# The first layer's four gate tiles as seven block products each, with their weight sums on GpSimd and their product sums on VectorE, and other hand-overs between stages

## The chip, the cores and the metric

The kernel runs on one core of a Trainium2 chip. The core has five engines that run side by side, each through its own instructions in order: TensorE (in the rows PE for its products and PEld for its weight loads), VectorE (DVE), ScalarE (ACT), GpSimd (POOL) and SyncE (SP), which here starts the transfers. The engines wait for one another by semaphores. The metric is the device time of one execution in microseconds (us); lower is better. All data are fp32, and in the rows every product of the program stands as two PE records, each with its own weight load.

## The reference, cut to what matters

Three different layers run one after the other over one sequence of 256 tokens of width 1024. The first projects a normalised, modulated input, runs a gated delta rule (4 heads) and a blockwise attention (8 heads), and merges both branches:

```python
gate_a, gate_b = sigmoid(h @ w_in[:, 4104:5128]), sigmoid(h @ w_in[:, 5128:6152])
merged = gate_a * (y_dn @ w_proj_dn) + gate_b * (y_mb @ w_proj_mb)
x = x + post_gate * rmsnorm(merged @ w_out)
```

The second has three branches (a linear recurrence, an mLSTM and a stick-breaking attention of 4 heads of width 64), three such gates, an output projection and a gated feed-forward part. The third has a neighbourhood attention, an RWKV-7 recurrence in both directions, an attention over a memory, and an expert feed-forward part with 16 experts, whose weights (16 x 3 matrices of 1024 x 2048 fp32) are read once.

## The kernel before

Tokens stand in two halves of 128 (t = 0, 1). `k.hT` holds the normalised input channel-major as 8 chunks of 128 channels by 256 tokens. Weights come through `k.ring`, six slots of 2 MB each, and sums are formed in the eight PSUM banks of `k.ps`.

The program is a row of stages. Each stage has one block of instructions for each engine; an engine ends its part with `k.finish`, which drains it and raises a semaphore, and `k.wait_finished` waits for named engines' earlier parts. `project` runs a stage's projections tile by tile from ring slots 0 and 1 (banks 0 to 3); TensorE's part began by waiting for VectorE, ScalarE and GpSimd.

Between a layer's projections and its merge stands a stage whose products depend on each other (`delta_and_attention` in the first layer, `memory_and_sticks` in the second). While VectorE and ScalarE work between two dependent products, TensorE takes pieces of the remaining gate projections. `fill.products` is a generator of these pieces; `spend(n)` takes the next n of them at places written out by hand, and `spend(1000)` at the end takes what is left.

In the first layer the generator was that of `GateFill`: four tiles of 512 columns, each as 4 blocks of 128 columns by 8 chunks of channels, so 32 products of 256 columns (tokens), 128 in all, one to a piece. Line 871 records them. `spend` took 108 pieces ahead of `turn_y`, the last dependent product of the stage, and 20 after it. ScalarE's `fill.copy` took each pair of blocks through a sigmoid out of PSUM (line 887).

In the second layer the generator was that of `SevenFill`: a tile is a 2 x 2 by 2 x 2 block product (two halves of the channels, two halves of the tile's columns, two halves of the tokens), and is formed from seven block products, p1 to p7, for eight, by Winograd's scheme. A block product is 4 chunks of channels by 2 blocks of 128 columns by 128 tokens. One piece is two products of 128 columns, a block product 4 pieces, a tile 28 and the four tiles 112 (line 973). It needs four sums of the token halves (`TokenSums`, s1 to s4, once, on GpSimd), four sums of the weight blocks of each tile (t1 to t4, `first_sums` and `later_sums`, 128x1024 each, on VectorE, in place in the ring slot), copies of three partial sums out of PSUM (`copy_product`: p1, p3, u2, on ScalarE), and six sums of products (`c11` and the five of `ends`, 128x256 each, on VectorE). The sigmoid follows on the finished tile (`sigmoid`, 128x1024).

At the end of `delta_and_attention`, VectorE (line 1807) and ScalarE (line 1841) copied the turned rows `yT`, which the merge multiplies. `first_merge` began on TensorE with a wait for VectorE and GpSimd, ran `branch_products` (8 steps of 8 products, four banks in turn, step i from 4 on waiting until VectorE has read step i-4), and between its second and third step `gate_rows`, after a wait for ScalarE. VectorE first forms the gain from two rows that SyncE loads after the whole stage before has ended (lines 671 and 672), and then merges (`merge_branches`). The weights of the second branch come into ring slot 1 when the fill's last tile has left it.

In `memory_and_sticks`, `values` formed the sticks' output with tokens on partitions (six products of 64 columns for each pair of heads), VectorE copied it, TensorE turned it (`turn_y(7, y_s)`, line 2143), and VectorE copied the turned rows (line 2249).

Of the kernel before, what the change touches and what calls it, by code (L numbers as in the profile page):

```python
# [17 lines left out]
ALU = mybir.AluOpType  # L18
# [304 lines left out]
def project(k, hT, stream, narrow=None, vector=None, between=None, sync=None, gpsimd=None, ahead=()):  # L323
# [37 lines left out]
    def _(pe):  # L361
# [134 lines left out]
class Merge:  # L496
# [7 lines left out]
    def __init__(self, k, name, branches, w_out, slots=(0, 1, 2, 3, 4), earlier=None, order=None):  # L504
# [35 lines left out]
def branch_products(k, pe, m, fill=None, beside=None):  # L540

    nc = k.nc
    for i, (p, b) in enumerate(m.order):
        if i < 2 and fill:
            fill.wait_read(pe, i)
        if i == 2 and beside:
            beside()
# [9 lines left out]
        for n in range(2):  # L557
            for c in range(br["chunks"]):
                last = nc.tensor.matmul(k.ps[:, i % 4, n * S:(n + 1) * S], w[:, c, (2 * p + n) * P:(2 * p + n + 1) * P], br["rows"](c),  # L559
                                        start=c == 0, stop=c == br["chunks"] - 1)  # L560
# [6 lines left out]
def merge_branches(k, dve, m):  # L567
# [3 lines left out]
    for i, (p, b) in enumerate(m.order):  # L571
# [7 lines left out]
        sums = k.ps[:, i % 4, :].rearrange("p (c s) -> p c s", s=S)  # L579
# [70 lines left out]
def first_merge(k, m, fill, tiles, ahead):  # L650
# [28 lines left out]
    def _(pe):  # L679
# [5 lines left out]
        k.wait_finished(pe, "vector", "gpsimd")  # L685
        branch_products(k, pe, m, fill, gate_rows)
# [21 lines left out]
        project_rows(mixed_tile, 0, 0, range(DC)).then_inc(first_done, 1)  # L708
        project_rows(narrow_tile, 1, 0, range(DC // 2))
        turn_normed(k, pe, m, 1)  # L710
        project_rows(narrow_tile, 1, 0, range(DC // 2, DC)).then_inc(first_done, 1)
        pe.wait_ge(m.hT_act, m.before["hT_act"] + 2)
        pe.wait_ge(m.hT_dve, m.before["hT_dve"] + 2)
        project_rows(mixed_tile, 2, 1, range(DC)).then_inc(k.tile_done[mixed_tile["slot"]], 1)
        project_rows(narrow_tile, 3, 1, range(DC)).then_inc(k.tile_done[narrow_tile["slot"]], 1)
# [25 lines left out]
    def _(act):  # L741
# [25 lines left out]
        for t in range(TT):  # L767
# [4 lines left out]
            nc.scalar.copy(rows[:, t, :].rearrange("p (g n) -> p g n", n=S)[:, 0::2, :], k.ps[:, 2 * t, :].rearrange("p (g n) -> p g n", n=S))  # L772
# [4 lines left out]
            nc.scalar.copy(k.small[:, t, 0:8], k.ps[:, 2 * t + 1, S:S + 8])  # L777
            nc.scalar.activation(rows[:, t, S:2 * S], k.ps[:, 2 * t + 1, 0:S], ACT.Sigmoid)
# [111 lines left out]
class TokenSums:  # L890


    def __init__(self, k):
        at = k.store[:, 0:4 * DC // 2 * P].rearrange("p (s c n) -> p s c n", s=4, c=DC // 2)
        self.s1, self.s2, self.s3, self.s4 = [at[:, n] for n in range(4)]
        self.ready = k.count["pools"] + 5
# [15 lines left out]
class SevenFill(GateFill):  # L912
# [141 lines left out]
    def sigmoid(self, k, act, i):  # L1054
        gate = self.tiles[i][2]
        self.vector_done(act, i, "ends")
        k.nc.scalar.activation(gate, gate, ACT.Sigmoid)

# [3443 lines left out]
```

## Time and profile before

| | us |
|---|---|
| median of 3 runs | 1985.04 |
| lowest, highest | 1982.36, 1987.23 |
| the profiled execution's own time | 1987.0 |
| its span, first to last instruction | 1985.2 |
| TensorE busy | 1680.0 (85%) |
| VectorE busy | 528.0 (27%) |
| ScalarE busy | 307.3 (15%) |
| GpSimd busy | 11.2 (1%) |

The first 41 us are the head, the first layer ends at about 336 us of the span, the second at about 746 us, the experts' loop of the third begins at about 1085 us and lasts to the end. A row's time stamp is counted from the first instruction. Busy shares are means over stages that differ: what a change is worth is read from the chain of work and the waits of the stage in which it is made.

### The profile page before, as it was taken

The numbers are of one execution on the slowest core, as the hardware profiler recorded it, in microseconds if no ns is written. First come the engines' busy times: TensorE is split into PE (matmuls) and PEld (weight loads), VectorE is DVE, ScalarE is ACT, GpSimd is POOL, SyncE is SP. The second block draws the span as 40 slices with busy tenths as digits, with TensorE's granted clock in tenths as the row PEclk, the third lists the DMA queues.
The fourth block names the chain that finished last, engine by engine and source line by source line (L and its number), as shares of the span: only waits on it lengthen the run. The fifth ranks groups of instructions, "written<-read, shape, count | busy, mean of one in ns | idle before, by whom it ended". The sixth has DMA issues, their size and how long they took to land.

```text
span 1985.2 us, 26212 instructions
## 1 busy us (share of the span) xinstructions
PE 1680.0 (85%) x11580; PEld 1066.2 (54%) x11580; DVE 528.0 (27%) x914; ACT 307.3 (15%) x594; POOL 11.2 (1%) x14
## 2 busy tenths in 40 slices
PE   6999999999999999999999966666776675666667
PEld 4868876899699648899886422222222221221222
DVE  1424422456455462355634000000000000000001
ACT  2150303332211111231421000000000000000001
POOL 1000001000000000000000000000000000000000
PEclk9999999999999999999999988878878877878879
DMA  8632380353396225403559999999999999999998
GB/s 312 226 123 80 126 297 3 129 187 136 115 317 200 76 95 182 159 2 76 173 201 389 403 430 432 432 433 433 432 430 430 432 431 432 433 433 432 431 430 338
DMA packets 109569, 558.54 MB, mean 281 GB/s; under 512 B 14312, under 2 KB 49197, under 8 KB 95789
## 3 DMA queue, kind: packets, MB, share of 16 engines
q1 hardware_dynamic: 108857, 556.09, 69.6%
q8 instruction: 69, 1.13, 0.2%
q10 hardware_dynamic: 628, 1.20, 0.2%
q14 instruction: 15, 0.12, 0.0%
HBM read 556.22 MB, written 1.05 MB: 281 GB/s over the span
## 4 chain that ended last, share of the span: by engine, by line
PE 63%; DMA 34%; DVE 1%; ACT 1%; issue 1%; ACTq 0%; SPq 0%; DVEq 0%; POOL 0%; POOLq 0%
DMA ring<-in_w_exp_up 17%; DMA ring<-in_w_exp_down 16%; PE ps L390 13%; PE ps L2414 7%; PE ps L871 6%; PE ps L4176 6%; PE ps L4128 4%; PE ps L559 4%; PE ps L600 4%; PE ps L2660 3%; PE ps L973 2%; PE ps L398 2%; PE ps L3238 1%; PE ps L700 1%; PE ps L3989 1%
## 5 line engine op out<-in xcount | busy, mean ns | idle before, releaser
L4176 PE MATMUL ps<-ring,xn 128*32 128x512 f32 x1984 | 306.5, 773 | 168.2 <-DMA ring<-in_w_exp_up 115.1
L4176 PEld LDWEIGHTS ps<-ring,xn 128*32 128x32 f32 x1984 | 71.0, 136 | 361.8 <-issue 182.2
L390 PE MATMUL ps<-hT,ring 128*128 128x256 f32 x1104 | 246.3, 383 | 1.8 <-ACTq L208 1.5
L4128 PE MATMUL ps<-ring,hT 128*32 128x512 f32 x960 | 146.8, 765 | 102.8 <-DMA ring<-in_w_exp_down 102.4
L390 PEld LDWEIGHTS ps<-hT,ring 128*128 128x128 f32 x1104 | 208.9, 191 | 33.2 <-issue 4.6
L4297 DVE TENSOR_TENSOR hT<-hT,ps 128x512 f32<-128x512 f32 x16 | 11.0, 687 | 564.5 <-PE ps L4176 564.5
L4128 PEld LDWEIGHTS ps<-ring,hT 128*32 128x32 f32 x960 | 34.2, 135 | 204.3 <-DMA ring<-in_w_exp_down 117.7
L871 PE MATMUL ps<-hT,ring 128*128 128x256 f32 x512 | 120.5, 384 | 0.4 <-issue 0.3
L871 PEld LDWEIGHTS ps<-hT,ring 128*128 128x128 f32 x512 | 93.7, 190 | 15.5 <-issue 3.4
L3989 PEld LDWEIGHTS ps<-xn,xs 128*128 128x128 f32 x512 | 62.0, 191 | 55.3 <-issue 54.6
L4235 ACT ACTIVATE hT<-ps 128x512 f32<-128x512 f32 x16 | 9.6, 597 | 447.0 <-PE ps L4176 447.0
L559 PE MATMUL ps<-chan,ring 128*128 128x256 f32 x352 | 76.9, 380 | 1.7 <-DVEq L208 0.9
L600 PE MATMUL ps<-ring,xn 128*128 128x512 f32 x176 | 76.5, 592 | 0.0
L4301 DVE COPY xn<-ps 128x512 f32<-128x512 f32 x16 | 11.1, 691 | 239.1 <-PE ps L4128 239.1
L559 PEld LDWEIGHTS ps<-chan,ring 128*128 128x128 f32 x352 | 66.6, 190 | 12.0 <-issue 2.0
L3989 PE MATMUL ps<-xn,xs 128*128 128x32 f32 x512 | 68.9, 278 | 0.5 <-DVE xn L4335 0.5
L2414 PE MATMUL ps<-xn,chan 128*128 128x128 f32 x528 | 62.6, 275 | 0.0
L2414 PEld LDWEIGHTS ps<-xn,chan 128*128 128x128 f32 x528 | 60.7, 192 | 0.0
L4123 PE MATMUL ps<-xn 128*128 128x512 f32 x128 | 59.3, 605 | 0.8 <-ACT xn L4243 0.8
L600 PEld LDWEIGHTS ps<-ring,xn 128*128 128x128 f32 x176 | 33.2, 190 | 39.4 <-issue 39.2
L4243 ACT COPY xn<-ps 128x512 f32<-128x512 f32 x16 | 9.4, 585 | 244.4 <-PE ps L4128 244.4
L4123 PEld LDWEIGHTS ps<-xn 128*128 128x128 f32 x128 | 22.8, 189 | 38.3 <-issue 37.7
(621 smaller groups left out, 1858.3 us busy)
## 6 DMA issues: line engine op xcount, KB each, us to landing
ring<-in_w_exp_gate SPq DMA_DIRECT2D x28, 4096.0 KB, 23.4
ring<-in_w_exp_up SPq DMA_DIRECT2D x28, 4096.0 KB, 25.3
ring<-in_w_exp_down SPq DMA_DIRECT2D x27, 4096.0 KB, 23.5
ring<-in_w_in SPq DMA_DIRECT2D x27, 2048.0 KB, 7.8
ring<-in_w_ffn_in SPq DMA_DIRECT2D x11, 2048.0 KB, 8.9
ring<-in_w_exp_gate SPq DMA_DIRECT2D x7, 2048.0 KB, 10.5
ring<-in_w_ffn_out SPq DMA_DIRECT2D x5, 2048.0 KB, 14.2
ring<-in_w_exp_up SPq DMA_DIRECT2D x5, 2048.0 KB, 13.7
```

Of the source, the lines that this page charges most:

```text
L390: last = nc.tensor.matmul(k.ps[:, 2 * slot + n // 2, (n % 2) * S:(n % 2 + 1) * S], wt[:, c, n * P:(n + 1) * P], src[:, c, 0:S], start=c == ...
L398: last = nc.tensor.matmul(k.ps[:, 2 * slot + t, 0:width], src[:, c, t * P:(t + 1) * P], wt[:, c, 0:width], start=c == 0, stop=c == chunks - 1)
L559: last = nc.tensor.matmul(k.ps[:, i % 4, n * S:(n + 1) * S], w[:, c, (2 * p + n) * P:(2 * p + n + 1) * P], br["rows"](c), start=c == 0, st ...
L600: product = k.nc.tensor.matmul(k.ps[:, 4 + 2 * t + h, :], m.mixed[:, c, t * P:(t + 1) * P], k.slot(slot, D)[:, c % 4, h * BANK:(h + 1) * B ...
L871: product = k.nc.tensor.matmul(k.ps[:, self.bank(unit), n % 2 * S:(n % 2 + 1) * S], w[:, c, n * P:(n + 1) * P], k.hT[:, c, :], start=c == ...
L973: last = k.nc.tensor.matmul(out[:, h * P:(h + 1) * P], weights[:, c, h * P:(h + 1) * P], rows[:, c, :], start=fresh and (c, h) == (0, 0), ...
L2414: last = nc.tensor.matmul(out[:, h * P:(h + 1) * P], weights_of[:, c, h * P:(h + 1) * P], rows_of[:, c, :], start=fresh and (h, c) == (0, ...
L2660: last = nc.tensor.matmul(k.ps[:, bank, :], rows_of[:, c, :], f.weights(k, at, 1)[:, 0, cols(h)], start=fresh and c == 0, stop=c == KH - 1 ...
L3989: last = nc.tensor.matmul(k.ps[:, bank, c * CAP:(c + 1) * CAP], picked[:, t, c, :], hot[:, t, :], start=t == 0, stop=t == TT - 1)
L4123: nc.tensor.matmul(k.ps[:, 2 * t + h, :], way[:, t * P:(t + 1) * P], y[:, h * BANK:(h + 1) * BANK], start=False, stop=True, skip_group_che ...
L4128: last = nc.tensor.matmul(k.ps[32 * i:32 * i + 32, Y + h, :], act_t[:, i, j, :], down_row(e, 2 * GATES + j, i, opening)[:, h * BANK:(h + 1 ...
L4176: last = nc.tensor.matmul(hidden_block(j, bank), xe[:, 2 * n + cc, :], hidden_columns(slot(e, q, EFF, opening)[:, cc, :], j), start=n == 0 ...
```

## The change

- The first layer's fill becomes a `PoolSevenFill`: seven block products for eight. Its `TokenSums` are made by GpSimd in the stage of the projections, and its weight sums by GpSimd in `delta_and_attention` (`make_sums`). VectorE forms the sums of products at places written out by hand between its other work, ScalarE's copies stand at such places too, and the four sigmoids stand at the end of ScalarE's part.
- `first_merge` starts its first step when `yT` is copied (`rows_ready`), and waits for VectorE and GpSimd only ahead of the second (`opened`); the merges of layers one and two take the banks in an order in which the first step's is free early. The same in `second_merge_and_ffn`.
- `project` of layers two and three waits for ScalarE only ahead of its second part (`scalar_from=1`); the rows projected at the end of the stage before stand in banks 4 to 7 for 0 to 3, and `ffn_out` drops a wait.
- The sticks: `values` forms the output turned, by four products (two of 256 and two of 128 columns) with 64 weight columns each, so that both heads of a pair fill the two halves of the partitions in alternation. `turn_y(7, y_s)`, its copy and their waits are gone. `sticks` issues the products of a pair of heads in alternation.

```diff
 def project(k, hT, stream, narrow=None, vector=None, between=None, sync=None, gpsimd=None, ahead=(), scalar_from=0):
...
-        k.wait_finished(pe, "vector", "scalar", "gpsimd")
+        k.wait_finished(pe, "vector", "gpsimd")
         for index, part in enumerate(stream.parts):
+            if index == scalar_from:
+                k.wait_finished(pe, "scalar")
...
+class PoolSevenFill(SevenFill):
+    SUMS = {name: n + 1 for n, name in enumerate(("t1", "t2", "t3", "t4"))}
...
+    def make_sums(self, k, pool):
+        for i, (slot, before, _) in enumerate(self.tiles):
+            w = [[self.weights(k, i, kh, j) for j in range(2)] for kh in range(2)]
+            pool.wait_ge(k.w_landed[slot], 16 * (before + 1))
+            if i:
+                self.product_done(pool, i - 1, "p5")
+            k.nc.gpsimd.tensor_tensor(self.t1, w[0][1], w[0][0], ALU.subtract).then_inc(k.pools, 1)
+            self.sum_done(pool, i, "t1")
+            k.nc.gpsimd.tensor_tensor(w[0][1], w[1][1], self.t1, ALU.subtract).then_inc(k.pools, 1)
+            self.product_done(pool, i, "p2")
+            self.sum_done(pool, i, "t2")
+            k.nc.gpsimd.tensor_tensor(w[0][0], w[0][1], w[0][0], ALU.subtract).then_inc(k.pools, 1)
+            k.nc.gpsimd.tensor_tensor(w[1][0], w[1][0], w[0][1], ALU.subtract).then_inc(k.pools, 1)
...
+    def first_block(self, k, dve, i):
+        self.product_done(dve, i, "p2")
+        self.copied(dve, i, "p1")
+        self.combine(k, self.place_of(i, 0, 0), self.place_of(i, 0, 0), self.blocks(k, i, 1), ALU.add, "c11")
...
 # delta_and_attention, GpSimd
         nc.gpsimd.memset(Y(0, 8)[high, :, 0:64], 0.0).then_inc(zeroed, 1)
+        pool.wait_ge(zeroed, 1)
+        fill.make_sums(k, pool)
 # VectorE
         nc.vector.tensor_tensor(d_y, d_y, over(k.const("chunk_ident"), 8), ALU.add).then_inc(triangles, 1)
+        fill.first_block(k, dve, 0)
         invert_vector(k, dve, d_t, a21_t, d_x, d_y, d_u, Y(0, 8), whole_done)
+        fill.ends(k, dve, 0)
...
         nc.vector.tensor_reduce(s.t1, squares, AX_X, ALU.add).then_inc(out_squares, 1)
+        fill.first_block(k, dve, 1)
...
         last.then_inc(y_ready, 1)
+        fill.ends(k, dve, 1)
+        fill.first_block(k, dve, 2)
         finish(0)
         shift(2)
         shift(3)
         weigh(2)
         weigh(3)
+        fill.first_block(k, dve, 3)
+        fill.ends(k, dve, 2)
         finish(1)
         dve.wait_ge(y_turned, 1)
-        nc.vector.tensor_copy(yT[:, 0:2, :], ...)
+        nc.vector.tensor_copy(yT[:, 0:2, :], ...).then_inc(y_ready, 1)
+        fill.ends(k, dve, 3)
         k.finish(dve, "vector")
 # ScalarE: fill.copy(0..7) give way to copy_product(0..3, "p1", "p3", "u2"), and at its end
         act.wait_ge(y_turned, 1)
-        nc.scalar.copy(yT[:, 2:4, :], ...)
-        fill.copy(k, act, 6)
-        fill.copy(k, act, 7)
+        nc.scalar.copy(yT[:, 2:4, :], ...).then_inc(y_ready, 1)
+        for i in range(4):
+            fill.sigmoid(k, act, i)
         k.finish(act, "scalar")
...
 # first_merge, TensorE (banks 4 to 7 for 0 to 3 in its project_rows)
-        k.wait_finished(pe, "vector", "gpsimd")
-        branch_products(k, pe, m, fill, gate_rows)
+        pe.wait_ge(*fill.rows_ready)
+        branch_products(k, pe, m, beside=gate_rows, opened=lambda: k.wait_finished(pe, "vector", "gpsimd"))
 # second_merge_and_ffn, TensorE
-        k.wait_finished(pe, "vector", "gpsimd")
...
-        branch_products(k, pe, m)
+        branch_products(k, pe, m, opened=lambda: k.wait_finished(pe, "vector", "gpsimd"))
...
 # memory_and_sticks, TensorE
         def values(g):
             pe.wait_ge(exps, g + 1)
             for n, h in enumerate((2 * g, 2 * g + 1)):
-                c = slice(n * 64, (n + 1) * 64)
-                d = slice(P + n * 64, P + (n + 1) * 64)
-                nc.tensor.matmul(k.ps[:, 4 + 2 * g, c], z[:, h, 0:P], v(0, h), start=True, stop=True)
-                nc.tensor.matmul(k.ps[:, 4 + 2 * g, d], z[:, h, P:S], v(0, h), start=True, stop=False)
-                last = nc.tensor.matmul(k.ps[:, 4 + 2 * g, d], z[:, h, S:W], v(1, h), start=False, stop=True)
+                nc.tensor.matmul(k.ps[64 * n:64 * n + 64, 4 + 2 * g, 0:S], v(0, h), z[:, h, 0:S], start=True, stop=False, skip_group_check=True)
+            for n, h in enumerate((2 * g, 2 * g + 1)):
+                last = nc.tensor.matmul(k.ps[64 * n:64 * n + 64, 4 + 2 * g, P:S], v(1, h), z[:, h, S:W], start=False, stop=True, skip_group_check=True)
             last.then_inc(sticks_done, 1)
...
         values(1)
-        spend(9)
-        pe.wait_ge(y_copied, 2)
-        turn_y(7, y_s)
         spend(1000)
 # VectorE
-            nc.vector.tensor_copy(y_s[:, :, g * P:(g + 1) * P], ...).then_inc(y_copied, 1)
+            nc.vector.tensor_copy(yT[:, 2 + g, :], k.ps[:, 4 + 2 * g, 0:S])
...
-        dve.wait_ge(y_turned, 2)
-        nc.vector.tensor_copy(yT[:, 2:4, :], ...)
         fill.ends(k, dve, 3)
```

## Rows read from the trace of the kernel before

**Rows 1.** Page, the chain that ended last, by engine.
```profile
PE 63%; DMA 34%; DVE 1%; ACT 1%; issue 1%; ACTq 0%; SPq 0%; DVEq 0%; POOL 0%; POOLq 0%
```
**Rows 2.** Stages: from:to, length, busy of each engine (instructions), clock, DMA share.
```profile
163.80:255.60 91.80, 91.52 (x824) 77.95 (x824) 44.97 (x83) 24.29 (x54) 0.00 (x0) 1.00 0.26 93
...
409.70:475.80 66.10, 65.31 (x580) 64.06 (x580) 43.64 (x73) 28.93 (x39) 0.00 (x0) 1.00 0.56 207
```
**Rows 3.** TensorE's waits: for whom, us in total, times, longest.
```profile
PE ps L390 <- ACTq L208: 1.5, 2, 0.9
...
PE ps L559 <- DVEq L208: 0.9, 1, 0.9
...
PE ps L871 <- issue: 0.3, 1, 0.3
PE ps L973 <- issue: 0.3, 1, 0.3
```
**Rows 4.** Chain in order of time, first layer: start, us, what.
```profile
166.28 5.62 PE ps L871 x26
...
214.47 0.44 PE ps L1699 x4
...
219.66 1.02 PE ps L1709 x16
...
227.23 8.83 PE ps L871 x40
...
246.78 8.63 PE ps L871 x40
255.42 0.37 issue
```
**Rows 5.** Chain in order of time, second layer's fill.
```profile
411.30 1.51 PE ps L2095 x16
412.81 6.45 PE ps L973 x56
...
459.86 0.17 PE ps L2135 x2
...
460.92 0.22 PE ps L2137 x2
461.14 6.31 PE ps L973 x56
...
472.81 0.45 PE ps L2143 x4
```
**Rows 6.** GpSimd in order of time: start, us, operation, shape [idle before].
```profile
336.66 1.26 POOL L905 TENSOR_TENSOR store<-hT 128x512 f32<-128x512 f32 x1
```
**Rows 7.** VectorE in order of time, first and second layer.
```profile
171.17 0.69 DVE L1750 TENSOR_TENSOR ring<-ring,constants 128x512 f32<-128x512 f32 x1
...
196.52 0.69 DVE L1754 COPY ring<-ps 128x512 f32<-128x512 f32 x1 [2.86 <-PE ps L1655]
...
203.00 0.69 DVE L1765 TENSOR_TENSOR ring<-xn 128x512 f32<-128x512 f32 x1
...
425.61 0.42 DVE L1013 TENSOR_TENSOR store<-store,ps 128x256 f32<-128x256 f32 x1 [0.58 <-PE ps L973]
```
**Rows 8.** ScalarE in order of time, a sigmoid of the second layer's fill.
```profile
438.42 1.28 ACT L1057 ACT_TABLE_LOAD   x1
439.71 1.06 ACT L1057 ACTIVATE tok<-tok 128x1024 f32<-128x1024 f32 x1
```
**Rows 9.** First merge: SyncE in order of time, the issue of a row.
```profile
256.60 0.43 SPq L672 DMA_DIRECT2D tok<-in_g_post  x1
```
**Rows 10.** First merge: VectorE in order of time.
```profile
266.72 1.22 DVE L722 TENSOR_TENSOR tok<-tok,ps 128x1024 f32<-128x1024 f32 x1 [19.21 <-DMA tok<-in_g_post]
...
269.12 1.28 DVE L582 TENSOR_TENSOR xn<-ps,tok 128x512 f32<-128x512 f32 x2
```
**Rows 11.** Third layer and experts, stretches as in rows 2.
```profile
980.00:1020.00 40.00, 40.00 (x243) 33.52 (x242) 15.47 (x31) 16.82 (x32) 0.00 (x0) 1.00 0.26 93
...
1060.00:1080.00 20.00, 20.00 (x79) 12.67 (x78) 6.21 (x10) 3.05 (x9) 0.00 (x0) 1.00 1.00 424
```

More of the change, by code:

```diff
@@ L320, in ahead, with project @@
         return loads
-def project(k, hT, stream, narrow=None, vector=None, between=None, sync=None, gpsimd=None, ahead=()):
+def project(k, hT, stream, narrow=None, vector=None, between=None, sync=None, gpsimd=None, ahead=(), scalar_from=0):
     nc = k.nc
@@ L545, in branch_products @@
             fill.wait_read(pe, i)
+        if i == 1 and opened:
+            opened()
         if i == 2 and beside:
@@ L1860, in first_layer @@
     head(k, x, stream.ahead())
-    fill = GateFill(k, "first_gates", [(w[0, :, 4104 + n * TILE:4104 + (n + 1) * TILE], k.gates(2, n // 2)[:, n % 2 * 4:n % 2 * 4 + 4, :]) for n in range(4)])
+    token_sums = TokenSums(k, before=0)
+    fill = PoolSevenFill(k, "first_gates", [(w[0, :, 4104 + n * TILE:4104 + (n + 1) * TILE], k.gates(2, n // 2)[:, n % 2 * 4:n % 2 * 4 + 4, :]) for n in range(4)], token_sums)
     s = FirstScratch(k)
     beside, counts = delta_inputs(k, s, (*stream.parts[0:3], stream.parts[5]))
-    project(k, k.hT, stream, narrow=(k.narrow_w[:, 0:64].rearrange("p (c n) -> p c n", n=8), k.small[:, :, 0:8], 8, k.w_landed[NARROW]), ahead=fill.loads[0:2], **beside)
+    project(k, k.hT, stream, narrow=(k.narrow_w[:, 0:64].rearrange("p (c n) -> p c n", n=8), k.small[:, :, 0:8], 8, k.w_landed[NARROW]), ahead=fill.loads[0:2],
+            gpsimd=lambda pool: token_sums.make(k, pool), **beside)
     k.advance(**counts)
+    k.advance(pools=4 + len(fill.SUMS) * len(fill.tiles))
     m = Merge(k, "first", [
@@ L1868, in first_layer @@
         {"rows": lambda c: k.chan[:, 4 + c, PAD:PAD + S], "w": k.ins["w_proj_mb"][0], "chunks": 4, "gate": k.gates(2, 1)},
-    ], k.ins["w_out"][0], order=[(p + q, b) for p in (0, 2) for b in range(2) for q in range(2)])
+    ], k.ins["w_out"][0], order=[(p + q, b) for p in (0, 2) for b in range(2) for q in range(2)], banks=(1, 3, 2, 0))
     causal = k.const("causal").rearrange("p (t n) -> p t n", t=TT)
@@ L2817, in _ @@
                 act.wait_ge(k.tile_done[first["slot"]], first["before"] + 2)
-            nc.scalar.copy(rows[:, t, 0:first["width"]], k.ps[:, t, 0:first["width"]])
+            nc.scalar.copy(rows[:, t, 0:first["width"]], k.ps[:, 4 + t, 0:first["width"]])
         k.finish(act, "scalar")
@@ L2856, in second_layer @@
     beside, counts = lru_and_weights(k, s, stream.parts[0:2], k.chan[:, 0:2, PAD:PAD + S], token_sums)
-    project(k, k.hT, stream, ahead=fill.loads[0:2], **beside)
+    project(k, k.hT, stream, ahead=fill.loads[0:2], scalar_from=1, **beside)
     k.advance(**counts)
@@ L4463, in third_layer @@
     beside, counts = rwkv_inputs(k, s, stream.parts[0:2], annex)
-    project(k, k.hT, stream, **beside)
+    project(k, k.hT, stream, scalar_from=1, **beside)
     k.advance(**counts)
```

84 lines of the change are left out of this document (54 added, 30 removed).

## The prediction

> **What bounds the kernel now.** I read the page's chain first: TensorE carries 63% of it and transfers 34% [rows 1]. The table of stretches then shows where the change lies: in both fill stages, 91.8 and 66.1 us long, TensorE is busy to within 0.8 us and in the first of them VectorE has half the stretch free and GpSimd all of it [rows 2]. So a piece of TensorE's work taken out there comes off the chain, and a wait put in there goes onto it. The list of TensorE's waits gives what hand-overs cost: 1.5 us for two starts of `project` behind ScalarE, 0.9 us for the second merge behind VectorE [rows 3]; the start of the first merge shows 0.37 us [rows 4]. A stage start on which nothing waits still shows 0.3 us [rows 3]. Last, does a gain this early reach the end? TensorE is full in 980 to 1020 us with transfers at 0.26 of their share, and transfers are full from 1060 us on [rows 11]; the experts' weights are started as TensorE leaves ring slots, so their stream starts earlier by whatever TensorE gains. I carry every gain to the end at its full size.
>
> **The fill.** A piece of `GateFill` is one product of 256 columns: 40 records, 20 pieces, in 8.83 us, 0.44 us each [rows 4]. A piece of `SevenFill` is two products of 128: 56 records, 14 pieces, in 6.45 and 6.31 us, 0.455 us each [rows 5]. There are 128 of the first and 112 of the second. The places of `spend` don't change, so 108 pieces stand ahead of the last dependent product, dearer by 0.015 us each, +1.6 us; and of the 20 behind it (8.63 us [rows 4]) 4 are left (1.8 us), -6.8 us. Net **-5.2 us**. With the dearest and cheapest of the four rows it is -3.7 to -5.9.
>
> The price of this is a set of new waits in TensorE's queue, where everything else of the stage stands behind them. I followed the order of pieces:
>
> - GpSimd's sums. Four 128x512 sums for the tokens took 1.26 us each [rows 6]; a weight sum has twice the elements, so 2.5 us by estimate, 10 us a tile. The token sums now run in the projections, where GpSimd did nothing. t1 and t2 of the first tile need only its landed weights. t3 and t4 wait for p2, piece 8, at about 168.5 us (the second run of pieces starts at 166.28 [rows 4]), and end near 173.5; they are wanted at pieces 21 and 25, which `spend` puts among the inverse's rounds, many microseconds later. The tightest place is tile 1: p2 ends near 203 us, where L1765 stands [rows 7]; t4 ends 5 us later, and piece 53 wants it some 10 us after p2. No wait, up to about 5 us a sum.
> - VectorE's sums. c11 is one 128x256 addition (0.42 us [rows 7]), `ends` five, 2.1 us. The first c11 stands ahead of work that waits for TensorE's next products; `ends` of tile 0 stands in the 2.86 us ahead of L1754 [rows 7], just inside. The others stand where VectorE waits for products. I take 0; without that cover each costs at most its length, 0.4 to 2.1 us.
> - ScalarE's copies replace eight sigmoids out of PSUM, and the switches of table between them. The four sigmoids at the end (1.06 us each after a 1.28 us load [rows 8]) end about 5.5 us after the copy of `yT`. TensorE then does its 4 pieces (1.8 us) and two merge steps (16 products of 256 columns, 7 us) before it asks for ScalarE: covered.
> - The gain rows. SyncE issues them only after ScalarE's end, so about 4 us later against the start of the merge than before. Before, VectorE began 10.1 us after that issue (256.60 to 266.72) and had read the first step at 269.8, 14 us after the merge began at 255.79 [rows 4, 9, 10]. Step 4 waits for that read; four steps and `gate_rows` are 36 times 256 columns, 15.8 us. If the landing takes as long after the issue, TensorE waits 2.2 us. But the rows were issued right behind 2 MB of the second branch's weights, and those now start at the merge's beginning with 4 us to run ahead: I take 0 and keep 2.2 for the range.
>
> What no row prices is VectorE and GpSimd at work on SBUF together: in the row of [rows 6] VectorE is all but idle. t3 and t4 of tile 0 (168.5 to 173.5) lie over the end of VectorE's chain to `triangles`, three operations of 0.69 us on SBUF and constants, of which L1750 ends at 171.86; TensorE's run of pieces ends at 171.90 [rows 4, 7]. There is no slack: what VectorE loses there TensorE waits. At 203 us the same holds nearly for L1765. The low end is 0. The high end is that VectorE's two-input work stands still while a sum runs: 3.6 us at the first place (three operations after 173.5), 1.5 to 3.3 us over the second, up to 6.9. I take **+1.0 us**, three operations longer by half, nearer to 0 because the operations that carry most of the stage (PSUM with one SBUF operand) are of another kind.
>
> The Trainium skill's GPSIMD Engine Reference (section "8. Key points") says that GpSimd shares its SBUF interfaces with VectorE and contends with its instructions that have two SBUF inputs. That speaks against this change; no run here shows it yet. By that rule, taken as full exclusion, the sum below would end at -1.5 us for -7.4.
>
> **The hand-overs.** Two `project` starts, 1.5 us, fall to 0.3 each: -0.9. The second merge, 0.9 to 0.3: -0.6; VectorE's end there (the last of `ends`, after the last piece) is covered by the first merge step, 4 products, 1.8 us. The first merge, 0.37 to 0.3: -0.1. Together **-1.6 us**; nothing if another wait takes each place, -2.7 if the gaps close altogether. The wait dropped in `ffn_out` shows no row, and I give it nothing.
>
> **The sticks.** `turn_y(7)` was 0.45 us of the chain [rows 5]. `values` took six pieces from 459.86 to 461.14, 1.28 us for a pair of heads [rows 5]. The new products have 64 weight columns in alternating halves of the partitions. Line 1709 is of that form: 8 products of 128 columns in 1.02 us, 0.13 each, where plain ones take 0.22 (two in 0.44) [rows 4]. Twice 256 and twice 128 columns then take 0.77 us; without overlap 1.32. I take the first, -0.5 a pair. The reordered `sticks`: line 2095, alternating halves of rows, takes 1.51 us for 8, 0.19 each for 0.22 [rows 5]; -0.1 for both. VectorE's second copy and its wait were behind the merge's start, counted above. Together **-1.55 us** (-0.4 to -1.9).
>
> **The sum.** -5.2 + 1.0 - 1.6 - 1.55 = -7.4 us. The profiled execution took 1987.0 us, with a span of 1985.2, so it would come to 1979.6. It is 2.0 us above the median of the three runs, 1985.04; against that median I predict **1977.6 us**. About 0.3% (6 us) is what a measurement of this kernel tells from no change.
>
> **The rivals.**
>
> - *VectorE is held off by GpSimd's sums.* For: no slack at 171.9 us, and the sums run in pairs. Against: most of VectorE's work there reads PSUM. It costs 3.5 to 7 us for 1.0, and the gain is 1.5 to 5 us: 1980 to 1983.5, no change by the bound. From a cost of 2.5 us on it decides. The skill's rule above is this one.
> - *GpSimd is too slow, and the change loses.* From t3 of tile 0 at 168.5 us to t4 of tile 3 there are 14 sums, and the last is wanted at about 248 us: 5.7 us each would fill that. Beyond it the end of the stage moves by 14 times the excess. At 6.7 us a sum, 2.7 times the estimate, the loss of 14 us exceeds the 8.4 us of gains by the bound: about 1991. Against: 1.26 us for half the elements, twice the price of VectorE (0.69), is a steady rate in four rows like that of [rows 6].
> - *A wait takes the place of those removed.* The gain rows land late (2.2 us), the next wait behind each start is as long, or a c11 comes late on ScalarE's in-order copies: 2 to 5 us back, 1980 to 1983, again no change.
>
> **How the numbers follow.** Forecast 0.57; held off 0.22; other waits 0.14; slower 0.07. The forecast's own range is 1975 to 1979. The range is 1974 to 1983.5, which leaves out the last case and little of the others; its low end is the fill's 5.9, hand-overs of 2.7, sticks of 1.9 with no loss on VectorE (10.5). Faster by over 0.3% has the first case, 0.57; within, the two middle ones, 0.36; slower 0.07.
>
> **What would show it.** The stretch from the fill's start to the first merge is 92.0 us before (163.8 [rows 2] to 255.8) and should be 87 to 88; the second fill's, with the start of its merge, shorter by 2.1; `project`'s two starts at 0.3. TensorE's list of waits should have no row for the fill's line 973 above 0.5 us. A wait of line 1078 on L1750, with that operation longer than 0.69 us, shows the first rival; waits of line 973 on GpSimd the second; L722 beginning over 12 us after the merge the third. The prediction is wrong if VectorE's or GpSimd's operations lengthen by more than half where they run together, or if the experts' stream does not start earlier by the sum.

## The result, and the profile after

The changed kernel takes 1989.66 us (median of 20 runs, 1987.1 to 1991.37) beside 1985.87 for the kernel before on the same chip: a ratio of 1.002 (95% interval 1.0014 to 1.0026), 3.8 us slower where 7.4 us faster was forecast. The profiled execution took 1989.14 us, its span 1987.4.

The table of stretches (columns as in [rows 2]) shows the two fill stages of the changed kernel, each from its first piece to the merge's first product:

```profile
162.90:257.20 94.30, 88.55 (x1016) 84.18 (x1017) 63.47 (x106) 20.45 (x56) 35.34 (x14) 0.96 0.26 90
411.60:475.90 64.30, 64.19 (x569) 62.02 (x569) 42.62 (x71) 28.89 (x39) 0.00 (x0) 1.00 0.57 213
```

The second stage fell from 66.2 us (409.73 to the merge's first product at 475.98) to 64.3, by 1.9 for the 2.1 that were forecast. The first rose from 91.9 to 94.3, where 87 to 88 was forecast: TensorE stands idle for 5.7 us of it, and its mean granted clock is 0.96 for 1.00. TensorE's list of waits (columns as in [rows 3]; "issue" stands for a gap in which TensorE waits for no other engine) names the place:

```profile
PE ps L1130 <- DVE ring L1805: 5.3, 1, 5.3
PE ps L392 <- issue: 1.2, 3, 0.5
PE ps L3442 <- issue: 1.2, 1, 1.2
...
PE ps L564 <- issue: 0.7, 2, 0.4
PE ps L978 <- issue: 0.5, 2, 0.3
...
PE ps L564 <- DMA ring<-in_w_proj_mb: 0.4, 1, 0.4
...
PE ps L1754 <- DVE ring L1840: 0.2, 1, 0.2
```

L1130 is the inverse's first product, L1805 the last operation of VectorE's chain to `triangles` (lines 1078 and 1750 before). VectorE in order of time, with that chain:

```profile
168.19 0.68 DVE L1802 COPY ring<-ps 64x512 f32<-64x512 f32 x1
168.91 2.03 DVE L1803 TENSOR_TENSOR ring<-ring,constants 128x512 f32<-128x512 f32 x1
170.87 2.82 DVE L1804 TENSOR_TENSOR ring<-ring,constants 128x512 f32<-128x512 f32 x1
173.73 2.71 DVE L1805 TENSOR_TENSOR ring<-ring,constants 128x512 f32<-128x512 f32 x1
176.36 0.41 DVE L1018 TENSOR_TENSOR tok<-tok,ps 128x256 f32<-128x256 f32 x1
```

and GpSimd beside it, with t3 and t4 of the first tile and t1 and t2 of the second:

```profile
167.66 2.73 POOL L1098 TENSOR_TENSOR ring<-ring 128x1024 f32<-128x1024 f32 x1 [9.72 <-PE ps L978]
170.36 2.79 POOL L1099 TENSOR_TENSOR ring<-ring 128x1024 f32<-128x1024 f32 x1
173.11 2.78 POOL L1093 TENSOR_TENSOR store<-ring 128x1024 f32<-128x1024 f32 x1
175.97 2.69 POOL L1095 TENSOR_TENSOR ring<-ring,store 128x1024 f32<-128x1024 f32 x1
```

Read the ends: the sums end at 170.39, 173.15 and 175.89; VectorE's three operations, 0.69 us each before [rows 7], end at 170.94, 173.69 and 176.44, each 0.55 us behind a sum. A sum that meets such an operation takes about 0.4 us longer than the 2.35 us of one that meets nothing. The copy out of PSUM (L1802), which runs inside the first sum, keeps its 0.68 us.

The wait has a tail. TensorE in order of time, and two stretches of it:

```profile
176.50 1.97 PE L1130 MATMUL ps<-ring 64*64 64x64 f32 x32 [5.34 <-DVE ring L1805]
178.40 1.22 PE L978 MATMUL ps<-store,ring 128*128 128x128 f32 x4
...
182.02 1.15 PE L1130 MATMUL ps<-ring 64*64 64x64 f32 x32
```

```profile
171.00:176.50 5.50, 0.16 (x3) 0.01 (x1) 5.47 (x3) 0.37 (x1) 5.42 (x3) 0.81 0.00 0
176.50:181.40 4.90, 4.90 (x69) 4.49 (x69) 1.54 (x4) 0.00 (x0) 2.16 (x1) 0.52 0.00 0
```

A round of 32 records takes 1.97 us there and 1.15 us later: behind the idle time TensorE works at the lower of its two levels (1.2 of 2.4 GHz) until about 181.4 us.

The sticks' `values` in the chain in order of time, for a pair of heads (1.28 us before, [rows 5]), and the gain rows' first reader in the first merge ([rows 10]):

```profile
461.72 0.58 PE ps L2206 x4
462.30 0.22 PE ps L2208 x4
```

```profile
269.97 1.22 DVE L727 TENSOR_TENSOR tok<-tok,ps 128x1024 f32<-128x1024 f32 x1 [12.15 <-DMA tok<-in_g_post]
```

To see where the rest went, the span is cut in three by the starts of unchanged products: the transposes ahead of the triangles (line 1642 before), and the last product kind of the third layer's projections (line 3096). Before: 165.2, 837.8 - 165.2 = 672.6, and 1985.2 - 837.8 = 1147.4 us. After: 164.3, 673.0 and 1150.1. So besides the 7.8 us missing in the middle part (-7.4 was forecast there), some 3 us are lost behind 837 us, where both programs have the same instructions (6844 records of products on TensorE in each).

### The profile page after: what moved, and what is told of

Same layout as the page of the kernel before. It is cut to its first block, busy times and chain, and to the rows that moved or that the text cites. A ratio compares the mean times of both kernels' runs of the same rounds, so it can differ in the third digit from the quotient of the medians.

```text
span 1987.4 us, 26648 instructions
## 1 busy us (share of the span) xinstructions
PE 1675.8 (84%) x11760; PEld 1070.3 (54%) x11760; DVE 546.7 (28%) x937; ACT 306.9 (15%) x599; POOL 56.2 (3%) x34
## 3 DMA queue, kind: packets, MB, share of 16 engines
q8 instruction: 70, 1.15, 0.2%
## 4 chain that ended last, share of the span: by engine, by line
PE 61%; DMA 35%; DVE 2%; issue 1%; ACT 0%; ACTq 0%; SPq 0%; POOL 0%; DVEq 0%; POOLq 0%
DMA ring<-in_w_exp_up 17%; DMA ring<-in_w_exp_down 16%; PE ps L392 13%; PE ps L2479 7%; PE ps L4240 6%; PE ps L978 5%; PE ps L4192 4%; PE ps L605 4%; PE ps L564 4%; PE ps L2725 3%; PE ps L876 3%; PE ps L400 2%; PE ps L3302 1%; PE ps L705 1%; DMA ring<-in_w_ada 1%
## 5 line engine op out<-in xcount | busy, mean ns | idle before, releaser
L392 PE MATMUL ps<-hT,ring 128*128 128x256 f32 x1104 | 246.4, 383 | 1.2 <-issue 1.2
L392 PEld LDWEIGHTS ps<-hT,ring 128*128 128x128 f32 x1104 | 208.9, 191 | 32.6 <-issue 4.0
L876 PE MATMUL ps<-hT,ring 128*128 128x256 f32 x256 | 59.1, 383 | 0.1
L876 PEld LDWEIGHTS ps<-hT,ring 128*128 128x128 f32 x256 | 47.3, 190 | 8.2 <-issue 2.2
L978 PE MATMUL ps<-store,ring 128*128 128x128 f32 x384 | 49.5, 280 | 0.0
L978 PE MATMUL ps<-hT,ring 128*128 128x128 f32 x384 | 47.8, 277 | 0.5 <-issue 0.5
```

What stands on the lines that cost most here:

```text
L392: last = nc.tensor.matmul(k.ps[:, 2 * slot + n // 2, (n % 2) * S:(n % 2 + 1) * S], wt[:, c, n * P:(n + 1) * P], src[:, c, 0:S], start=c == ...
L876: product = k.nc.tensor.matmul(k.ps[:, self.bank(unit), n % 2 * S:(n % 2 + 1) * S], w[:, c, n * P:(n + 1) * P], k.hT[:, c, :], start=c == ...
L978: last = k.nc.tensor.matmul(out[:, h * P:(h + 1) * P], weights[:, c, h * P:(h + 1) * P], rows[:, c, :], start=fresh and (c, h) == (0, 0), ...
```

## The experiments

Each kernel's median is given beside that of the kernel before on the same chip, as a ratio with its 95% interval. "Middle" and "tail" are the second and third part of the span, worked out as above.

| kernel | median us | ratio | middle | tail |
|---|---|---|---|---|
| before, two profiles | 1985.45 to 1985.97 | | 672.6, 672.6 | 1147.4, 1146.5 |
| changed, three profiles | 1989.66, 1989.5 | 1.002, 1.002 | 673.0, 673.0, 672.8 | 1150.1, 1151.5, 1151.4 |
| hold, two profiles | 1981.24, 1978.64 | 0.998, 0.9966 | 665.4, 665.6 | 1147.9, 1146.3 |
| split | 1982.27 | 0.9986 | 666.2 | 1148.8 |
| rest | 1984.08 | 0.9991 | 669.9 | 1145.5 |
| no_handovers | 1988.86 | 1.0013 | 674.1 | 1144.6 |
| after_warm | 1982.36 | 0.9988 | 671.1 | 1143.9 |
| hold_warm | 1978.97 | 0.9966 | 665.4 | 1147.0 |
| before_warm | 1985.61 | 1.0001 | 672.6 | 1143.7 |
| after_tiny6 | 1985.78 | 1.0002 | 672.6 | 1146.7 |
| after_tiny16 | 1986.88 | 1.0007 | 672.8 | 1146.6 |
| probe_two, one execution | 1996.45 | | 679.7 | 1149.0 |
| probe_one, one execution | 1988.72 | | 673.9 | 1147.7 |

The middle repeats within 0.3 us. The tail of a single execution doesn't: that of before_warm is 3 us shorter than before's at the same median, and the two probes, whose TensorE program is that of before, end at 1147.7 and 1149.0 us for its 1146.5 and 1147.4. So a tail counts where several profiles or the median say the same.

**hold: the sums moved out of VectorE's way.**

```diff
             self.sum_done(pool, i, "t2")
+            if i == 0 and hold:
+                pool.wait_ge(*hold)
             k.nc.gpsimd.tensor_tensor(w[0][0], w[0][1], w[0][0], ALU.subtract).then_inc(k.pools, 1)
...
-        fill.make_sums(k, pool)
+        fill.make_sums(k, pool, (triangles, 1))
```

> The changed kernel, with t3 and t4 of the first tile held on GpSimd until VectorE's chain to `triangles` has ended. Theory A (a VectorE operation with two SBUF inputs that meets a GpSimd sum stands still until that sum has ended): lines 1803 to 1805 take 0.69 us each again for 2.03, 2.82 and 2.71, TensorE's wait of 5.3 us is gone, and with it the granted clock of 0.50 behind it (about 2.2 us); the stretch from the fill's start to the first merge falls from 94.3 to 86.5 to 87.5 us, the whole by 7 to 7.5 us. VectorE's operations of the inverse, with one input in PSUM, keep their 0.42 us beside the sums. Theory B (the two engines share a bandwidth): the sums then lengthen the inverse's operations as they did the chain's, and less than half of the 7.5 us comes back. Theory C (the loss beyond 746 us has to do with this wait): the stretch beyond 746 us also gets back its 3 us, and the whole falls by 10.

Measured: 0.998 (0.9971 to 0.9988), 8.4 us below the changed kernel's median. VectorE's chain and the first sum behind it, in order of time:

```profile
171.04 0.69 DVE L1805 TENSOR_TENSOR ring<-ring,constants 128x512 f32<-128x512 f32 x1
171.65 0.68 DVE L1806 TENSOR_TENSOR ring<-ring,constants 128x512 f32<-128x512 f32 x1
172.37 0.70 DVE L1807 TENSOR_TENSOR ring<-ring,constants 128x512 f32<-128x512 f32 x1
```

```profile
173.24 2.35 POOL L1100 TENSOR_TENSOR ring<-ring 128x1024 f32<-128x1024 f32 x1 [12.87 <-DVE ring L1807]
```

No row of TensorE's waits names the inverse any more, the stretch from the fill's start to the merge is 251.87 - 165.03 = 86.8 us, and the sums' 2.35 us beside VectorE's operations with one input in PSUM (0.89 us for two, as before) show that these do not meet. Theory A holds, B falls. The tail is 2 to 5 us shorter than the changed kernel's too, as theory C had it; by the medians, less the middle, it is about 1 us in the first comparison and 3 in the second. That the wait alone is not the reason of a long tail, after_tiny6 and after_tiny16 show: they keep it.

**split: shorter instructions on GpSimd.** Each sum as four of 128x256, nothing held:

```diff
+            for c in range(DC // 2):
+                last = k.nc.gpsimd.tensor_tensor(out[:, c, :], a[:, c, :], b[:, c, :], ALU.subtract)
```

> The changed kernel, nothing held, each GpSimd sum of 128x1024 as four of 128x256. Theory A (VectorE is held for the length of one GpSimd instruction): a quarter takes about 0.6 us (2.35 / 4), so lines 1803 to 1805 take at most 1.3 us each, and TensorE waits 1 to 2 us for 5.3; whether the clock falls behind so short a wait is open, 3.3 to 6.5 us come back. Theory B (shared bandwidth, as much data as before): the three operations stay at 2 to 2.8 us each, and the wait stays at 5 us.

Measured: 0.9986 (0.9977 to 0.9995). A quarter took 0.72 us where it met nothing, and VectorE's chain:

```profile
168.67 1.09 DVE L1807 TENSOR_TENSOR ring<-ring,constants 128x512 f32<-128x512 f32 x1
169.68 1.21 DVE L1808 TENSOR_TENSOR ring<-ring,constants 128x512 f32<-128x512 f32 x1
170.93 1.10 DVE L1809 TENSOR_TENSOR ring<-ring,constants 128x512 f32<-128x512 f32 x1
```

TensorE waits 1.2 us for 5.3, the clock stays 1.00 behind it, and the middle gets back 6.8 us, a little more than the 6.5 that were expected at most. As much data is summed, so it is the length of one GpSimd instruction that VectorE is held for, not a share of a bandwidth. The Trainium skill says so, on its page SBUF — State Buffer, section "SBUF: two separate sides": VectorE and GpSimd have one pair of ports in common, as an exclusive lock for a whole instruction, which VectorE wants with two SBUF inputs. The trace agrees in each end time above, and adds that the two then take turns.

**probe_two and probe_one: the meeting alone.** The kernel before, with `GateFill`, and three GpSimd instructions that read `hT`, behind `a_turned`:

```diff
+        pool.wait_ge(a_turned, 1)
+        for n in range(3):
+            nc.gpsimd.tensor_tensor(spare[:, n], k.hT[:, 0:4, :], k.hT[:, 4:8, :], ALU.subtract)   # probe_two
+            nc.gpsimd.tensor_copy(spare[:, n], k.hT[:, 0:4, :])                                    # probe_one
```

> The kernel before, with three GpSimd differences of two SBUF tensors (128x1024 each, 2.35 us by the trace after, whose results nobody reads) put behind the transposes of the first layer, at about 166.3 us, beside VectorE's chain of lines that copy out of PSUM and combine SBUF with constants. Theory A (a VectorE operation with two SBUF inputs stands still until the running GpSimd instruction has ended, then goes, and GpSimd's next one waits for it): the first 64x512 combination ends 0.55 us after the first difference, the second 0.55 us after the second one, the first 128x512 after the third; the copies out of PSUM between them keep 0.68 us; TensorE's wait at the inverse's first product, 0 before, is 3 to 5 us, and the granted clock behind it drops. Theory G (it was the fill's own use of the ring slot, read by TensorE, written by GpSimd, not the engines' meeting): these differences read and write other tensors, so VectorE keeps 0.69 us and TensorE does not wait.

> As the probe with differences, but GpSimd makes three copies of 128x1024, with one SBUF input each. If VectorE is held by any GpSimd instruction that reads and writes SBUF, TensorE waits 2 to 5 us as there (less if a copy is shorter than 2.35 us). If the two inputs on GpSimd's side are what takes the share of SBUF that VectorE wants, VectorE's operations keep 0.69 us and TensorE does not wait.

Measured, one execution each: 1996.45 and 1988.72 us beside 1985.7; middle 679.7 and 673.9 us for 672.6. VectorE with the differences:

```profile
168.51 1.61 DVE L1750 TENSOR_TENSOR ring<-ring,constants 64x512 f32<-64x512 f32 x1
170.13 2.75 DVE L1751 TENSOR_TENSOR ring<-ring,constants 64x512 f32<-64x512 f32 x1
172.89 0.68 DVE L1752 COPY ring<-ps 64x512 f32<-64x512 f32 x1
173.61 2.02 DVE L1753 TENSOR_TENSOR ring<-ring,constants 128x512 f32<-128x512 f32 x1
175.55 0.68 DVE L1754 TENSOR_TENSOR ring<-ring,constants 128x512 f32<-128x512 f32 x1
```

and with the copies:

```profile
167.80 1.26 DVE L1750 TENSOR_TENSOR ring<-ring,constants 64x512 f32<-64x512 f32 x1
169.07 1.44 DVE L1751 TENSOR_TENSOR ring<-ring,constants 64x512 f32<-64x512 f32 x1
```

With three sums that nothing needs, the kernel before shows a wait at the same place (4.3 us) and the same clock behind it (0.50). The held operations end 0.55 us behind the first, second and third sum, as theory A had it. Theory G falls. A copy, with one input, holds VectorE as well; at 1.04 us it holds it for less, TensorE waits 1.4 us, and the clock stays 1.00.

**after_warm: the wait without the clock.** Six products of 512 columns ahead of the wait for `triangles`:

```diff
         spend(13)
+        for _ in range(6):
+            nc.tensor.matmul(k.ps[:, 6, :], k.const("ident"), k.hT[:, 0:2, :]..., start=True, stop=True)
         pe.wait_ge(triangles, 1)
```

> The changed kernel with six products of 512 columns, read by nobody, put on TensorE ahead of its wait for `triangles`, where it stood idle for 5.3 us. At 0.85 us each by line 4090 (two records in 0.85 at full clock) they fill 5.1 us. Theory H (the half clock in 176.5 to 181.4 us follows from the idle time): the granted clock stays 1.00, the first two rounds of the inverse take 1.08 to 1.15 us each for 1.97 and 1.91, and the stretch from the fill's start to the first merge falls from 94.3 to about 92.1 us; the wait for line 1805 shrinks to 0 to 0.5 us, but the time up to 176.5 us stays. Rival: the clock falls all the same (it has another cause, the sums on GpSimd or the kind of work), and the stretch stays at 94.3.

Measured: 0.9988 (0.9978 to 0.9997). TensorE in order of time:

```profile
170.78 5.32 PE L1701 MATMUL ps<-hT,constants 128*128 128x512 f32 x12
176.29 1.15 PE L1130 MATMUL ps<-ring 64*64 64x64 f32 x32 [0.19 <-DVE ring L1807]
```

From the transposes to the first product that uses the inverse (line 1655 before) 35.9 us pass, 38.0 in the changed kernel, 30.5 in hold, 30.2 before. So theory H holds here: of the 7.5 us between the changed kernel and hold 5.4 are the wait, and 2.1 the half clock that follows from it. The whole is 6.9 us below the changed kernel, each beside the kernel before (-3.1 and +3.8), and that is more than the 1.9 us of the middle: the tail is 1143.9 us. So the tail got shorter together with a change that stands 660 us ahead of it, which after_tiny6 and after_tiny16 look into.

**rest and no_handovers: the parts of the change apart.** rest is the kernel before with the hand-overs and the sticks, no_handovers the changed kernel without the hand-overs of layers two and three.

```diff
-    project(k, k.hT, stream, scalar_from=1, **beside)    # no_handovers: taken back, with banks 0 to 3
+    project(k, k.hT, stream, **beside)
```

> The kernel before, with the hand-overs and the sticks alone: its first layer's fill and the start of its first merge are unchanged. By the traces before and after, up to 746 us: two starts of `project` -0.6 (0.61 to 0.37 and 0.86 to 0.48), second merge -0.7 (0.94 to 0.26), sticks -1.3, so -2.6 us at the start of the third layer. Theory D (what the change loses beyond 746 us, about 3 us, comes from the hand-overs in layers two and three): the whole is within 0.5 us of before. Theory E (it is where TensorE's gaps without a wait and the granted clock behind them happen to lie, which moves with the program): the whole is 1 to 4 us faster than before, and the gaps named issue lie at other lines than in either trace.

> The changed kernel without the hand-overs of layers two and three: the first layer's fill, the start of its merge, and the sticks are the change's. The fill's loss stays (the stretch 94.3 us for 91.9), the sticks' gain too (-1.3). Theory D (the loss beyond 746 us comes with the hand-overs): 0.5 to 1.5 us slower than before. Theory E (it is where gaps and the clock behind them lie): anywhere from 0 to 5 us slower than before, with other places of the gaps.

Measured: 0.9991 (0.9978 to 1.0003) and 1.0013 (1.0003 to 1.0023). The middle parts are as the traces said: 669.9 - 672.6 = -2.7 us for rest, +1.5 for no_handovers. Neither tail (1145.5 and 1144.6 us) is longer than before's. By the medians, less the middle, both would be 1 to 2 us longer, with intervals as wide as that, so these two runs speak against theory D and do not settle it. The two tiny runs below do: they keep every hand-over, and the 3 us are gone.

**before_again, after_again, after_third: is the tail chance?** The two kernels again, unchanged.

> The kernel before once more, for a second profile. Theory E (the stretch beyond 835 us scatters between executions of one program: gaps named issue, the granted clock behind them): against the first profile the gaps lie elsewhere or have other lengths, and the time from the end of the projections (line 3096, 837.8 us) to the first experts' piece of line 4128 (1112.8 us), 275.0 us there, differs by over 1 us. Theory F (the program fixes it): the same places, 275.0 us within 0.5.

> The changed kernel once more, for a second profile. The first layer's wait of 5.3 us on line 1805 and the clock of 0.50 behind it come again. Theory E (scatter): the time from the end of the projections of the third layer (837.3 us) to the first experts' piece of line 4192 (1114.8 us), 277.5 us in the first profile, differs by over 1 us. Theory F (the program fixes it): 277.5 us within 0.5, with the gap of 1.2 us on line 3442 and the half clock on the first pieces of line 4240.

> The changed kernel once more, with its median beside that of the kernel before on one chip. By theories L and T: 1150 to 1151 us from line 3096 to the end of the span a third time, and 1.001 to 1.003 of before. By scatter between executions: that stretch more than 2 us off 1150.5, and a median anywhere from 0 to 4 us above before.

Measured: one execution of 1986.97 and one of 1992.25 us, and for the third 1989.5 us, 1.002 (1.0012 to 1.0029). By the mark that the expectations named, the kernel before took 274.1 us for 275.0, the changed one 281.1 for 277.5, where its first experts' pieces stood at half clock for longer. To the end of the span the two profiles of before agree within 0.9 us and the three of the changed kernel within 1.4, 3 to 5 us above. With the probes, before's TensorE program scatters by 2.5 us in four executions, and the highest is 1.1 us below the changed kernel's lowest. The medians (+3.8 and +3.5 us) repeat the difference too, so most of it is not scatter between executions, against theory E; the experts' first pieces scatter (below).

**after_tiny6 and after_tiny16: more records, no time.** Six or sixteen products of 16 columns in the same idle time as in after_warm:

```diff
+        for _ in range(6):
+            nc.tensor.matmul(k.ps[:, 6, 0:16], k.const("ident"), k.hT[:, 0, 0:16], start=True, stop=True)
         pe.wait_ge(triangles, 1)
```

> The changed kernel with six products of 16 columns, read by nobody, in TensorE's idle time ahead of `triangles`: 0.12 us each, 0.7 us of 5.3, so nothing behind them moves in time, but 12 records more stand ahead of all later code. Theory H (the half clock follows from the idle time): 0.7 us of thin work do not keep the clock up, and the stretch from the fill's start to the first merge stays at 94.3 us. Theory L (where TensorE's gaps without a wait fall depends on the count of instructions ahead): the stretch from line 3096 to the end is 1143 to 1149 us as in the other programs, the whole 1 to 4 us below the changed kernel. Theory T (the time at which the third layer begins decides): 1150 to 1151 us, and the whole as the changed kernel.

> As the one with six, with sixteen (32 records, 1.9 us by 0.12 each). Theory L: another place again, 1143 to 1149 us from line 3096 to the end, and gaps of other lengths than with six. Theory T: 1150 to 1151 us, as the changed kernel.

Measured: 1.0002 (0.9991 to 1.0012) and 1.0007 (0.9999 to 1.0016), 3.7 and 2.6 us below the changed kernel on the same chip. The products took 1.4 and 3.6 us together, twice what was expected, so that waits of 4.1 and 1.9 us were left. The middle does not move and the clock behind the idle time still falls (0.50), but the tails are 1146.7 and 1146.6 us, with line 3096 at 838.4 and 838.8 us (837.3 to 839.0 in the changed kernel). So theory T falls, and the shorter tail that theory L forecast came. Most of it lies in the recurrence of the third layer; the stretch from its line 3394 (before's number) to line 3595, in the changed kernel,

```profile
911.90:961.20 49.30, 47.17 (x838) 43.17 (x834) 24.37 (x35) 9.60 (x23) 0.00 (x0) 0.90 0.49 131
```

and with six small products ahead, in the same columns, with TensorE's wait in it:

```profile
913.50:959.20 45.70, 44.45 (x837) 40.47 (x834) 24.33 (x35) 9.60 (x23) 0.00 (x0) 0.96 0.53 141
```

```profile
PE ps L3444 <- issue: 0.3, 1, 0.3
```

The same records take 49.3 us at a mean clock of 0.90 with a gap of 1.2 us (L3442 above), and 45.7 us at 0.96 with one of 0.3. Here is that gap in the changed kernel's chain in order of time, and the transfers named instruction in 926 to 932 us of it (packets, MB, share), of which the first began at 927.92 us:

```profile
928.92 0.35 PE ps L3442 x11
929.27 1.20 issue
930.47 0.50 PE ps L3442 x9
```

```profile
q8 instruction: 2, 0.03, 2.6%
```

The traces tell where such gaps fall. Count TensorE's records: products, weight loads and the control instructions between them. Then every gap named issue of 0.25 us or more in the recurrence, apart from the 0.26 us at its start, stands at record 10435 or 12739 where TensorE's program is that of before, at 12482 in rest, and at 12994 (12995 in one run) or 14019 in all others. Each number leaves 194 or 195 when it is divided by 256. With sixteen products more ahead the gap at 14019 stays at that count and falls on other code (L3418 there, L3444 with six). And in every profile such a gap ends 2.2 to 2.9 us after a transfer of 16 KB on the queue q8 has begun. In the Trainium skill, on the page Advanced Engine Details and Errata, section "ISA Cache", a cache line of instructions is 16 KB, which are 256 instructions. The traces agree with that. So TensorE very likely waits there for its next instructions, and the count of records ahead decides on which code that falls.

It doesn't decide what the tail costs. hold and split have the changed kernel's TensorE program, record for record, with gaps of 1.1, 0.6 and 1.2 us at record 14019 for its 1.2, and their tails are 1146.3 to 1148.8 us for its 1150.1 to 1151.5. So theory L holds for the place of the gaps; that it accounts for the 3 us is not shown, and what does is open.

**hold_warm, before_warm, hold_again: the first experts' pieces.** Three products, read by nobody, in the waits of the expert choice:

```diff
+            idle(BANK if bank == CHOSEN_PLACES else S)
             pe.wait_ge(k.vectors, ready)
...
+        idle(S)
         pe.wait_ge(k.vectors, HOT)
```

> The held version, with three products read by nobody (512, 256 and 256 columns) in TensorE's waits of the expert choice, in 1078 to 1085 us of its trace. Theory H (the half clock at the first experts' pieces, where 16 records of the up or gate products took 3.1 to 3.4 us for 1.92, follows from the thin work ahead of it): the first pieces run at 1.00, and the time from them to the end falls from 893.8 to 892.6 us, the whole by 1.2 us at most, less what the products themselves delay (up to 0.9 us where the clock has already fallen). Rival: the drop only moves by a microsecond or two, and the time stays or rises by 0.5 to 1.5.

> The kernel before, with the same three products in the expert choice. In its two profiles the half clock fell on 1085 to 1089 us, under a wait for VectorE, and the first experts' pieces ran at 1.00. By theory H nothing is to be had: within 0.5 us of before by the trace from the first piece on, and 0 to 0.9 us later at that piece. Rival: if the phase is chance, the half clock now falls on the first pieces and costs 1.2 to 2.3 us.

> The held version once more. Beside before: 0.998 again (-3 to -5.5 us). Its second profile tells how much of the stretch behind the third layer's projections (1121.4 us from there to the end of the span in its first profile, by 1953.3 - 831.8 for the last up product) is fixed by the program: by scatter 1 to 3 us off, fixed by the program within 0.5.

Measured: hold_warm 0.9966 (0.9954 to 0.9978), hold_again beside it the same, 0.9966 (0.9954 to 0.9978), before_warm 1.0001 (0.9992 to 1.0011), with its first pieces at full clock as before. In the two profiles of hold and in that of hold_warm, the first 16 records of the experts:

```profile
1085.86 3.17 PE L4242 MATMUL ps<-ring,xn 128*32 128x512 f32 x16
```

```profile
1084.57 1.92 PE L4242 MATMUL ps<-ring,xn 128*32 128x512 f32 x16
```

```profile
1084.63 3.62 PE L4246 MATMUL ps<-ring,xn 128*32 128x512 f32 x16
```

The first two are one program in two executions: whether the half clock falls on these records or on work ahead of them that is waited for anyway is chance, 1.25 us between these two. The added products did not keep the clock up there; that expectation of theory H failed, and what would is open.

## Why the prediction was wrong

- **The fill, -5.2 us: right.** In hold, where the sums are out of the way, the stretch is 86.8 us for 91.9, -5.1. The sums on GpSimd take 2.35 us where they meet nothing (2.5 was the estimate); no wait of TensorE names them.
- **The meeting of VectorE and GpSimd, +1.0 us: this step failed.** The prediction had the place (no slack at 171.9 us) and both mechanisms, and took "three operations longer by half". Measured are 7.5 us (38.0 - 30.5). Three things were off. VectorE does not slow, it stands still until the running sum has ended: the first rival was the right one, and its price (3.5 to 7 us) still fell short. GpSimd did not stop after t4: t1 of the second tile waits only for a product that was already done, so the third operation was held too, 5.3 us for the 3.6 of the high end. And the half clock behind the wait, 2.1 us, was no term at all. At the second place (1.5 to 3.3 us feared) VectorE lost more, 2.2 us on line 1840 alone, but TensorE had pieces of the fill to do, and waited 0.2 us (the row of L1840).
- **The hand-overs, -1.6 us: half right.** `project`: its three starts show 1.2 us of issue; before they showed 1.5 [rows 3] and one row more, `PE ps L390 <- issue: 0.3, 1, 0.3`; so -0.6 for -0.9. Second merge: 0.94 to 0.11 us between the fill's last and the merge's first product, -0.8 for -0.6. First merge: 0.26 for 0.37, but TensorE then waits 0.4 us for the second branch's weights (w_proj_mb above), so +0.3 for -0.1; the gain rows, feared with 2.2 us, came 12.7 us after the merge's start, later than the 12 us named as the third rival's sign, and stopped nothing. Together -1.1 for -1.6.
- **The sticks, -1.55 us: right but for 0.1.** `values` 0.80 us for 1.28 (0.77 forecast), `turn_y` gone; the reordered `sticks` gave nothing.
- **Every gain carried to the end at full size: wrong by 3 to 4 us**, and not for the reason that was looked at. The experts' stream does start earlier by what is gained ahead of it: in hold's two profiles its first transfer of up weights is issued at 1016.6 and 1015.7 us for 1023.8, the third layer's projections having ended 6.0 and 7.0 us earlier. But the changed kernel takes 3 to 4 us longer over the same instructions behind them. With 12 or 32 records of products more on TensorE that loss is gone, and in hold, with none more, it is smaller. The gaps named issue, 0.3 to 1.2 us long, are at most a part of it, and its cause is open.

Together: 6.5 us in the meeting of VectorE and GpSimd (7.5 for 1.0), 1.2 in the other steps of the middle part (hold's -7.2 for -8.4) and 3 to 4 in the tail, against the 11.2 us between forecast and medians. The held version comes to -4.5 and -6.8 us in its two comparisons, -7.2 and -7.0 in the middle, less 2.7 and 0.2 elsewhere, for one and the same program. It is the version to take; it beats both kernels in both.

## What to carry to other kernels

Before moving work to GpSimd, list VectorE's operations with two SBUF inputs on the critical path while it would run (and small ones from SBUF to SBUF, below): each can be held for a whole GpSimd instruction, so hold the instruction back by a semaphore until that chain is through, or cut it into short ones. Price a new wait of TensorE with the half clock behind it, and try whether cheap products in the idle time keep it up. A difference of 3 us in 2000 between two programs may lie in code that neither changed, and one program can differ by 2 us between two comparisons: compare the stretches ahead of it and behind it apart.

## What was not expected of the hardware

- One GpSimd instruction held VectorE's 0.69 us operations to 2.0 to 2.8 us, and was held in return by only 0.4; operations with one input in PSUM kept 0.42 and 0.68 us beside it. Line 1840, whose second input is a small table of statistics, took 2.84 us for 0.69. Line 1835, a product of such a table with a constant, SBUF to SBUF with one input, took 1.06 us for 0.17 beside a sum and ended with it.
- A wait of 5.3 us cost TensorE 2.1 us more in half clock behind it, and one of 4.3 us brought the same clock; waits of 1.2 and 1.4 us at the same place cost nothing more.
- In the third layer's recurrence TensorE stood still for 0.3 to 1.2 us with no engine to wait for, always at a record whose number leaves 194 or 195 when divided by 256, and went on 2.2 to 2.9 us after a transfer of 16 KB on an instruction queue had begun.
- With twelve more records in idle time the median was 3.7 us lower on the same chip; the count of records alone is not the reason, since hold has the changed kernel's.
